# The modulation vectors of an adaLN trunk: three sections as VectorE columns, the last one in four TensorE visits

## The reference

```python
def trunk(x, c, g_norm, w_ada, b_ada, g_final, even_p, odd_p):
    for l in range(DEPTH):                                   # DEPTH = 2
        mod = jax.nn.silu(c) @ w_ada[l] + b_ada[l]           # (1, 3 * 1024)
        shift, scale, gate = jnp.split(mod, 3, axis=-1)
        h = rmsnorm(x, g_norm[l]) * (1 + scale[:, None, :]) + shift[:, None, :]
        out = even_mixer(h, ...) if l % 2 == 0 else odd_mixer(h, ...)
        x = x + gate[:, None, :] * out
    return rmsnorm(x, g_final)
```

## Time and profile before

| | |
|---|---|
| time, median of three runs | 1484.58 us (1484.26 to 1485.5) |
| profiled execution: device time | 1484.11 us |
| profiled execution: span | 1482.0 us |
| granted TensorE clock, mean | 0.998 of full speed |
| TensorE busy | 1447.9 us, 98% |
| VectorE / ScalarE / GpSimd busy | 851.2 / 669.4 / 367.3 us |

### The profile page before, as it was taken

The page is one execution under the profiler, slowest core; times in us unless marked ns, Lnnn a source line. Parts: engine busy times, 40 slices in busy tenths (PEclk is TensorE's granted clock), DMA queues, the critical chain, the costliest instruction groups (busy, mean ns, idle before and its releaser), DMA issues.

```text
span 1482.0 us, 18893 instructions
## 1 busy us (share of the span) xinstructions
PE 1447.9 (98%) x7162; PEld 1114.5 (75%) x7162; DVE 851.2 (57%) x1523; ACT 669.4 (45%) x1161; POOL 367.3 (25%) x455
## 2 busy tenths in 40 slices
PE   8999999999999999999999999999999999999997
PEld 5677765688787787787888887568878778787885
DVE  7533345754796517885443434576589652789423
ACT  3323436744443435543543343775443343555332
POOL 2011023431200022765210002352220002376311
PEclk9999999999999999999999999999999999999999
DMA  9566742124333331116334444212433233111531
GB/s 384 205 217 212 259 135 86 58 60 139 107 100 100 104 104 55 44 29 241 89 97 156 136 121 108 99 44 72 147 115 100 87 107 107 51 43 33 181 100 71
DMA packets 54618, 174.27 MB, mean 118 GB/s; under 512 B 6000, under 2 KB 7408, under 8 KB 52224
## 3 DMA queue, kind: packets, MB, share of 16 engines
q1 hardware_dynamic: 54528, 173.07, 35.7%
HBM read 149.94 MB, written 23.10 MB: 117 GB/s over the span
## 4 chain that ended last, share of the span: by engine, by line
PE 83%; DVE 8%; ACT 4%; DMA 2%; issue 2%; POOL 1%; SPq 0%; DVEq 0%; ACTq 0%; POOLq 0%
PE ps L561 22%; PE ps L563 21%; PE ps L562 21%; PE ps L1116 3%; PE ps L1152 3%; PE ps L1171 2%; DVE w_lo L543 1%; PE ps L1675 1%; PE ps L1658 1%; PE ps L303 1%; PE ps L1709 1%; PE ps L1190 1%; PE ps L1499 1%; PE ps L1133 1%; ACT w_hi L531 1%
## 5 line engine op out<-in xcount | busy, mean ns | idle before, releaser
L543 DVE TENSOR_TENSOR w_lo<-at,w_hi 128x1024 fp32r<-128x1024 f32 x160 | 201.0, 1256 | 344.5 <-ACT w_hi L531 344.5
L531 ACT ACTIVATE w_hi<-at 128x1024 fp32r<-128x1024 f32 x162 | 169.5, 1047 | 140.4 <-PE ps L563 131.7
L561 PE MATMUL ps<-h_e_hi,w_hi 128*128 128x512 f32 x464 | 182.8, 394 | 4.7 <-DVE w_lo L543 4.7
L562 PE MATMUL ps<-h_e_lo,w_hi 128*128 128x512 f32 x464 | 180.7, 389 | 0.0
L563 PE MATMUL ps<-h_e_hi,w_lo 128*128 128x512 f32 x464 | 180.6, 389 | 0.0
L561 PE MATMUL ps<-h_a_hi,w_hi 128*128 128x512 f32 x384 | 153.6, 400 | 2.1 <-DVE h_a_lo L593 1.3
L562 PE MATMUL ps<-h_a_lo,w_hi 128*128 128x512 f32 x384 | 149.7, 390 | 0.0
L563 PE MATMUL ps<-h_a_hi,w_lo 128*128 128x512 f32 x384 | 149.6, 390 | 0.0
L561 PEld LDWEIGHTS ps<-h_e_hi,w_hi 128*128 128x128 f32 x464 | 87.1, 188 | 28.3 <-issue 8.3
L563 PEld LDWEIGHTS ps<-h_e_hi,w_lo 128*128 128x128 f32 x464 | 87.1, 188 | 18.3
L562 PEld LDWEIGHTS ps<-h_e_lo,w_hi 128*128 128x128 f32 x464 | 87.1, 188 | 18.1 <-issue 0.5
(11 more groups left out here) (289 smaller groups left out, 3000.0 us busy)
## 6 DMA issues: line engine op xcount, KB each, us to landing
at<-blocks_in SPq DMA_DIRECT2D x162, 512.0 KB, 3.7
at<-w_ada SPq DMA_DIRECT2D x32, 512.0 KB, 4.6
at<-w_ada SPq DMA_DIRECT2D x8, 1024.0 KB, 18.4
at<-xs SPq DMA_DIRECT2D x4, 2048.0 KB, 9.9
z_kept<-at SPq DMA_DIRECT2D x32, 256.0 KB, 2.1
at<-z_kept SPq DMA_DIRECT2D x32, 256.0 KB, 2.8
sg_kept<-at SPq DMA_DIRECT2D x16, 256.0 KB, 4.5
at<-sg_kept SPq DMA_DIRECT2D x16, 256.0 KB, 2.6
```

Of the source, the lines that this page charges most:

```text
L531: act.activation(whi[:, n % PAIRS, :, cols], wring[:, n % SLOTS, :, cols], ACT.Copy).then_inc(sem("w_hi"), 1)
L543: dve.tensor_tensor(wlo[:, n % PAIRS], wring[:, n % SLOTS], whi[:, n % PAIRS].bitcast(F32), ALU.subtract)\
L561: pe.matmul(o, stationary[0], moving[0], start=first, stop=False)
L562: pe.matmul(o, stationary[0], moving[1], start=False, stop=False)
```

## The change

- **Parts 1 and 2 are gone** as sixteen TensorE steps, with their four evictions, turns and adds.
- **Three sections** (layer 0 gate, layer 1 shift and scale: 24 groups of 128 outputs, t = 0..23) are computed on VectorE. The weights come transposed, 128 outputs by 1024 inputs, 512 KB per t (`late_load`). Silu(c) of group g lies replicated on all 128 partitions (`srep[g]`: a broadcast DMA of c, then Silu on ScalarE in iteration 1). `late_column(t, g)` is one scalar_tensor_tensor of 128x1024, weight times `srep[g]`, with the sum over the free axis as accumulator output: 48 of them. After each section VectorE adds the bias, at the end it also makes the scale columns.
- **Where the columns stand**: `LATE_AT` gives one t to each of the iterations 2..23 but 16, and two to 12, 13 and 14. In its iteration, column (t, 0) stands before the split of block b + 2, column (t, 1) behind it. In 12 to 14 the second t's two columns come behind that.
- **Slots**: t < 16 alternate between two slots of 512 KB; from t = 16 on there is one slot (the other's place is needed by the up-projection weights), so the load of t waits for column (t - 1, 1).
- **The last section** (layer 1 gate) stays on TensorE: four visits, behind blocks 3, 5, 8 and 11, each with two k-chunks of four matmuls of 128x256; two transposes behind block 12.
- **SyncE**: in the prelude `late_load(0)` and the broadcast of c wait until four steps of part 0 are done; the rest of the constants and the weights of block 2 stand behind this wait. In iteration b the order is: bias tables, broadcast of c for g = 1 (b = 1), `late_load`, `gate_load`, `stream_weights`, store of the gate block. Before, each `ada_load` stood at the same place.
- **ScalarE** waits at the start of phase b for all of the modulation; before, it did so at the end of phase b.

```diff
+    LATE_AT = [b for b in range(2, B_OUT0 - 1) for _ in range(0 if b == B_KR else 2 if 12 <= b < 15 else 1)]
+    ONE_SLOT = 16
+    GATE_AT = (3, 5, 8, 11)
+    def late_slot(t):
+        return t % 2 if t < ONE_SLOT else 0
+    def late_load(sp, t):
+        uses = late_uses(t)
+        if len(uses) > 1:
+            sp.wait_ge(sem("late_col"), G * (uses[-2] + 1))
+        sp.dma_start(late_w[late_slot(t)], w_late[t]).then_inc(sem(f"ada_in{late_slot(t)}"), 16)
+    def late_column(dve, t, g):
+        if g == 0:
+            dve.wait_ge(sem(f"ada_in{late_slot(t)}"), 16 * (1 + len(late_uses(t))))
...
+        if t or g:
+            dve.wait_ge(sem("late_col"), G * t + g)
+        l, c = divmod(2 * DC + t, 3 * DC)
+        w = late_w[late_slot(t)].rearrange("p (h w) -> p h w", h=2)
+        dve.scalar_tensor_tensor(w if g else unread, w, 1.0, srep[g].rearrange("p (h w) -> p h w", h=2), ALU.mult, ALU.mult,
+                                 accum_out=mod[:, l, c, g:g + 1]).then_inc(sem("late_col"), 1)
+    def gate_step(pe, v):
+        for e in range(2):
+            k = 2 * v + e
+            pe.wait_ge(sem(f"ada_in{2 + 3 * e}"), 16 * (v + 2))
+            for q in range(4):
+                last = pe.matmul(ps(ADA_BANK)[32 * q:32 * q + G, 0:2 * P], siluc[:, G * k:G * k + G], gate_w[e][:, 2 * P * q:2 * P * (q + 1)],
+                                 start=(k == 0), stop=(k == DC - 1))
+        last.then_inc(sem("ada_used"), 1)
...
     def p_sync(sp):
...
-        ada_load(sp, 0)
+        sp.wait_ge(sem("ada_used"), 4)
+        late_load(sp, 0)
+        sp.dma_start(srep[0], c_in[0:1, :].to_broadcast([P, D])).then_inc(sem("ada_in3"), 16)
...
         def a_sync(sp):
...
-                if g == 0 and b in ADA_AT and ADA_AT[b] + 1 < ADA_STEPS:
-                    ada_load(sp, ADA_AT[b] + 1)
+                if g == 0:
+                    if b == 1:
+                        sp.wait_ge(sem("h_lo"), DC)
+                        sp.dma_start(srep[1], c_in[1:2, :].to_broadcast([P, D])).then_inc(sem("ada_in4"), 16)
+                    for t in range(1, LATE):
+                        if LATE_AT[t] - 1 == b:
+                            late_load(sp, t)
+                    if b + 1 in GATE_AT:
+                        gate_load(sp, GATE_AT.index(b + 1))
                 stream_weights(sp, b + 1)
...
         def a_tensor(pe):
...
-                    if b in ADA_AT:
-                        ada_step(pe, 1 + ADA_AT[b] // DC, ADA_AT[b] % DC,
-                                 [ada_q[q // 2][:, q % 2 * T:(q % 2 + 1) * T] for q in range(4)])
...
+                if g == 0 and b in GATE_AT:
+                    gate_step(pe, GATE_AT.index(b))
+                if g == 0 and b == GATE_AT[-1] + 1:
+                    gate_turn(pe)
...
         def a_vector(dve):
...
+                todo = [t for t in range(LATE) if LATE_AT[t] == b] if g == 0 else []
+                for t in todo[:1]:
+                    late_column(dve, t, 0)
                 dve_split(dve, b + PAIRS)
+                for t in todo:
+                    if t > todo[0]:
+                        late_column(dve, t, 0)
+                    late_column(dve, t, 1)
+                    if (t + 1) % DC == 0:
+                        late_section(dve, t)
...
         def a_scalar(act):
...
+                if g == 0 and b == 1:
+                    for n in range(G):
+                        act.wait_ge(sem(f"ada_in{3 + n}"), 32)
+                        act.activation(srep[n], srep[n], ACT.Silu).then_inc(sem("p_silu"), 1)
...
         def b_scalar(act):
+            if g == 0:
+                act.wait_ge(sem("mod_set"), MOD_SET)
```

More of the change, by code:

```diff
@@ new lines, in gate_step, with gate_turn @@
+    def gate_step(pe, v):
+        for e in range(2):
+            k = 2 * v + e
+            pe.wait_ge(sem(f"ada_in{2 + 3 * e}"), 16 * (v + 2))
[3 more added lines that the diff above has]
+        last.then_inc(sem("ada_used"), 1)
+    def gate_turn(pe):
+        pe.wait_ge(sem("ada_ev"), 2)
+        for n in range(2):
+            last = pe.transpose(ps(ADA_BANK)[:, n * P:(n + 1) * P], gate_out[:, n * P:(n + 1) * P], ident)
+        last.then_inc(sem("ada_T"), 1)
@@ L392, in p_tensor @@
         for k in range(DC):
[L393 to L394 removed]
+            pe.wait_ge(sem(f"ada_in{k}"), 16)
+            ada_step(pe, k)
             if k == 5:
```

149 lines of the change are left out of this document (80 added, 69 removed).

## The result

| | before | after |
|---|---|---|
| time, median | 1485.04 us (1484.26 to 1485.58) | 1504.22 us (1501.76 to 1506.41) |
| ratio after / before, 95% interval | | 1.0125 (1.0101 to 1.0149) |
| profiled execution: device time / span | 1484.11 / 1482.0 us | 1504.38 / 1501.5 us |
| granted TensorE clock, mean | 0.998 | 0.989 |

What follows compares the result with a forecast made beforehand. TensorE, busy 98% of the span, was taken as the bound. Its 15.7 us gain against 17.4 given back, plus tables (1.0) and late landings (0.8), made +3.5 us: 1488 us, range 1480 to 1496 for 8 in 10.

Steps and rivals of the forecast that it cites:

- own gain of TensorE: Steps, waits and turns removed from TensorE, 21.2 us, less visits and transposes added, 5.5: 15.7 us gained.
- (a): First visit, behind block 3: its loads queue behind other transfers, so it ends later; 2.4 us given back.
- (b): The other visits: loads for the one behind block 8 queue up, the other two have more time; 1.5 us.
- (c): Iterations 12 to 15: VectorE's backlog delays the copy of block 15 and the split of block 17; 4.1 us.
- (d): Iterations 18 to 23, one slot: cycle of load, column, split, column takes 7.4 us against 5.45 per block; 7.3 us.
- (e): End of phase a: the late last split delays the last gate store and phase b's first VectorE operation; 2.1 us.
- tables, late landings: Columns lengthened beside bias tables, 1.0 us, and loads landing later than 3.6 us now and then, 0.8 us.
- the case of the missing parallelism: Visits: their four column groups don't run side by side, 2.4 us each, +4.4; counted within "Port and queue".
- three signs: Prediction fails if columns are far from 1.28 us, one-slot loads land under 3 us, or phase b has unseen slack.
- VectorE keeps pace: Rival: in iterations 18 to 23 each column's load arrives before it is missed; 1478.6 us, chance 0.15.
- The slots don't stack up: Rival: columns of 1.22 and landings of 3.5 us shorten the one-slot cycle to 7.2; about 1484.5 us, chance 0.20.
- Port and queue: Rival: GpSimd stops columns for whole instructions, visits cost 2.0 us each, landings are longer; 1494 us, chance 0.15.

Runs made afterwards that it cites:

- e_store_b: Second run of the e_store kernel, beside e_nav2 and e_two_c_b: 1471.93 us, ratio 0.9903.
- e_store: e_two_c with the last gate store issued ahead of the ring load that waits for VectorE: 1468.97 us, ratio 0.9899.
- e_gate_early: The change with visits behind blocks 4, 7, 9 and 11 and their loads issued one iteration earlier: 1494.61 us, ratio 1.0068.
- e_nav2: e_store with the change's own column placement in iterations 12 to 17 and its one slot for t = 16 and 17: 1475.24 us, ratio 0.9925.
- e_slot2: The change with a second slot for columns from t = 18 on, unread results moved to a PSUM bank: 1491.34 us, ratio 1.0046.
- e_two_c_b: Second run of the e_two_c kernel, without the early last store, beside e_store_b: 1474.42 us, ratio 0.9919.
- e_two: The change with early visit loads, later visits, two slots to the end, splits before both columns and columns of iterations 13 to 17 re-placed: 1478.63 us, ratio 0.9957.
- e_two_c: e_two with the broadcast of c for g = 1 issued before the two up-projection weights: 1475.13 us, ratio 0.9934.
- e_fill: The change with filler matmuls of constants, results unread, on TensorE at most of its phase a waits: 1497.06 us, ratio 1.0082.
- e_floor: The change with columns 8 wide, one late load per slot, and three of four visits and half the fourth left out: 1472.26 us, ratio 0.9920.
- e_hold: The kernel before, with VectorE delayed by unread dependent multiplications in front of two splits, iterations 8 and 19: 1495.99 us, ratio 1.0079.
- e_nav: The change with columns re-placed: two t in iterations 10, 12 and 14, none in 15, one in 13 and 16: 1504.89 us, ratio 1.0130.
- e_noload: The change with full-width columns but only the first late load of each slot: 1486.22 us, ratio 1.0006.

## Why the prediction was right in sign and wrong in size

| step | forecast, us | measured, us | by |
|---|---|---|---|
| own gain of TensorE | -15.7 | -13.3 | e_store_b, some 2.5 of small waits for columns still in it (e_store, the same kernel in another set: -15.9) |
| (a), (b) visits | +3.9 | +9.6 | e_gate_early |
| (c) iterations 12 to 15 | +4.1 | +3.3 | e_nav2 - e_store_b |
| (d) one slot, (e) last store | +9.4 | +12.9 | e_slot2 |
| last store behind the ring load, as before | 0 | +2.5 | e_two_c_b - e_store_b |
| broadcast of c in front of a split | 0 | +3.5 | e_two - e_two_c |
| tables, late landings | +1.8 | in the rows above | |
| sum | +3.5 | +18.5 | +19.2 measured |

The parts were measured in different surroundings and sets and add up within a microsecond. With waits that hide each other, and an own gain of -13.3 or -15.9 by the set, that is luck; what the table shows is which terms were too small.

**The step that failed is that a wait of TensorE was priced at its own length.** The sum has no term for the clock, though it sends TensorE into some eight waits of 1 to 4 us. The waits themselves were forecast well: in phase a the change has 6.2 us for the visits' weights against 3.9, 3.48 + 1.60 in step (c) against 4.1, and 0.59 + 1.62 + 2.18 + 2.33 in (d) against 7.3, together 18.0 against 15.3. What the sum lacks is the lower clock, up to 11.9 us by TensorE's busy time. e_fill gives 4.4 (start of phase b) to 7.2 us (medians) of it back; the start of attention has up to 3.4, and the lateness goes from +14.9 to +19.3 between the rotary products and the second layer. There a wait for ScalarE has grown from 1.05 to 2.23 us. I had costed what is queued behind ScalarE's new wait for the modulation at nothing. Late columns alone don't explain it: e_floor, with columns 8 wide and 15 us ahead of the kernel before at the start of phase b, waits 2.23 us there too, and e_store_b, with the early last store, not at all. Which part ScalarE's own order has in it was not tried apart and stays open. The trace before gave a hint that I did not use: its clock stays at 1.00 where TensorE has no wait, which is a reason to ask what it is with waits.

**(b) was mis-sized.** I gave the visits behind 5 and 11 "an iteration more". All four loads are issued one iteration ahead: for the one behind 5 that was 8.6 us before the visit, and it didn't wait; for the one behind 11 it was 5.7 us before block 11 ended, behind a column load that waits for its slot. The visit behind 3 waited 2.15 + 0.35 us (forecast 2.4), the one behind 8 1.69 + 0.66 (forecast 1.5), the one behind 11 the remaining 1.3 of the six waits' sum of 6.2 (forecast 0). With up to 1.7 us of clock behind each of the first and the second this comes to 9.6, as much as e_gate_early gives back; but that kernel has the wait for block 4's `w_lo` instead of the first and a shorter dip at the start of attention, so the equality is chance.

**(d) was right in kind and a little short in its load.** The cycle exists and e_slot2 removes it: 5.45 us between splits instead of 7.7. Its load took 4.4, 3.8, 4.3, 3.8, 4.5 and 4.3 us where I took 3.6 from a quiet stretch; that makes 0.6 x 4 = 2.4 us more. A block's load is issued right behind each of them and shares the engines; that this is the reason is argued only. With (e), forecast at 2.1 and by the stores' times 2.4 (issued 5.24 us behind the start of phase b instead of 2.86), this makes 11.8 of the 12.9; the windows at 192 to 200 (up to 1.7 us of clock) and part of the dip at the start of attention are the nearest candidates for the rest.

**The broadcast** was listed as a transfer, and its waiter, ScalarE, was left out: done as in step (e), where what is queued behind ScalarE's wait is named, the working would have come to the split of block 4.

**Right, and shown:** the gain of the removed steps; the free step behind block 1; a column's 1.26 for 1.28 us; a visit of 1.0 to 1.2 us at the full clock as one old step (the four column groups run side by side), so the case of the missing parallelism fell; the waits in all of the places (a) to (e); the first VectorE operation of phase b behind the store of 219.54. Block 0 starts at 39.73 us against 39.47, and at 39.73 in e_hold too, which has the old prelude, so the moved wait of the prelude cost nothing there. None of the three signs by which the prediction was to fail came: the columns took what was forecast, no load in the one slot landed under 3 us, and phase b had no slack. They did not cover what it left out.

**The rivals.** "VectorE keeps pace" fell with the cycle read in the chain. "The slots don't stack up" fell, landings were longer and not shorter. "Port and queue" had the queue right (late visits, longer landings) and the port wrong: columns beside bias tables took up to 1.76 instead of 1.22 us, but 48 of them with a mean of 1.26 leave some 2 us for all of it, on VectorE and not on the path throughout. The same holds for the forecast's higher estimate, 1491, with whole columns and tables shutting each other out: a table did take 2.98 us instead of 1.30 beside a column,

```profile
84.95 2.98 POOL L846 TENSOR_TENSOR at<-at,at 128x256 f32<-128x256 f32 x2 [59.63 <-DMA at<-rpb_pad]
...
85.70 1.76 DVE L317 SCALAR_TENSOR_TENSOR at<-at,at 128x1024 f32<-128x1024 f32 x1
```

while a table beside an idle VectorE took 1.31 us (at 109.44 and 128.12). So the two do hold each other up, and it was mostly GpSimd that paid, which had time. The forecast's estimate of 1485.6 fell the other way: these loads are slower than its 3.2 us and than 3.6. (It also took the shorter load for six cycles, where step (d) has four that count.)

**Open.** Why some waits of about 2 us lower the clock and others don't. The single 2.33 us of e_hold and the one at 208.64 in the change left it alone, the 2.15 + 0.35 in front of a visit did not. The same wait before block 4 did both in two kernels; first e_floor, then e_gate_early, with the matmul behind it:

```profile
68.04 0.64 PE L641 MATMUL ps<-h_a_hi,w_hi 128*128 128x512 f32 x1 [2.18 <-DVE w_lo L623]
68.48 0.63 PE L642 MATMUL ps<-h_a_lo,w_hi 128*128 128x512 f32 x1
...
67.68 0.47 PE L637 MATMUL ps<-h_a_hi,w_hi 128*128 128x512 f32 x1 [2.19 <-DVE w_lo L619]
67.99 0.40 PE L638 MATMUL ps<-h_a_lo,w_hi 128*128 128x512 f32 x1
```

Nothing here tells the cause. The clock's dip around 40 us, in the prelude, came in 12 of the 15 profiles with the changed prelude and in neither of the two with the old one (the kernel before and e_hold); whether the change makes it is not shown. As short as in the change it costs little: block 2 starts at 54.49 us with it, at 54.36 without it in e_gate_early. In the profiles of e_nav and e_two_c the prelude's clock was low for 10.2 and 13.7 us, and block 2 started at 57.37 and 58.12; that lies in the spread of their times. e_noload's 6 us above its forecast are told by its waits, not by a run of their own.

## What to carry to other kernels

A wait that a change puts in front of TensorE costs its length and can cost half of the time at the lower clock behind it as well, so a forecast needs a term for both; here the second was up to 11.9 us beside 18.0 us of waits in phase a. A load into a single buffer that is used up in the same iteration makes a cycle (load, all that is done with it, next load): compare its length with the iteration's before anything else, and take the load's time from a stretch with as many transfers as there will be. In an in-order queue, of DMA issues as of instructions, list for each wait what stands behind it, and put first what the critical engine asks for: here moving loads, visits, a store, a broadcast, a split and a few columns and giving the columns a second buffer to the end, with all of the work as it was, turned 1.25% slower into 1.0% faster.

## What the runs showed of the hardware

- TensorE's clock fell to 0.50 behind 4.79 us of waiting (e_hold) and to 0.59 and 0.55 in the two 4 us windows behind 3.48 + 1.60. It stayed at 1.00 behind single waits of 2.33 and 2.19 us (e_hold, e_gate_early) and fell behind one of 2.18 (e_floor). Matmuls whose result nobody reads held it at 1.00 (e_fill).
- A 512 KB load took 3.6 us alone and 3.8 to 4.5 with another right behind it; the second of a visit's loads took 11.3, behind two up-projection weights (768 and 1024 KB), a broadcast, a block's load, a column's load and the visit's first.
- A multiplication with sum over 128x1024 float32 took 1.22 to 1.26 us, so the sum costs nothing to speak of; beside a GpSimd table it took 1.76 and the table 2.98 instead of 1.30.
- Two SyncE loads whose buffers were free waited behind one whose slot was not, for so long that TensorE stood still for 4.90 us (e_nav).
